# Decoder trunk with experts on one core: another order of the value tiles, an eleven-step choice of experts, slots released behind a second round, parameters fetched in attention

## What is computed

```python
for l in range(DEPTH):                       # DEPTH = 2, 256 tokens, width 1024
    h = rms_norm(x, norm1_g[l])
    proj = h @ w_in[l]                       # 1024 -> 3072: q, k, v of two attention groups
    o_da = diff_attention(q, k, v, lam)      # softmax(a) - lam * softmax(b), causal
    o_sb = stick_breaking_attention(...)     # log-sigmoid scores with a reverse cumulative sum
    x = x + concat([norm(o_da), norm(o_sb)]) @ w_out[l]
    h2 = rms_norm(x, norm2_g[l])
    x = x + hierarchical_moe(h2, ...)        # best group of 4, then the best two of its 8 experts
                                             # expert: (silu(h2 @ w_gate) * (h2 @ w_up) * weight) @ w_down
```

## Time and profile before

| | |
|---|---|
| median of 3 runs | 782.0 us (781.1 to 782.14) |
| the profiled execution, its own time | 780.52 us |
| its span, first to last instruction | 778.7 us |
| PE, DVE, ACT busy | 671.7, 306.5, 127.3 us |
| mean granted TensorE clock | 0.949 of full |
| bytes moved by DMA | 240.10 MB, mean 308 GB/s |

### The profile page before, as it was taken

One profiled execution on the slowest core, in us unless ns is written; L12 is line 12 of the kernel. 1 busy time (PEld: TensorE's weight loads), 2 busy tenths in 40 slices (PEclk: granted clock), 3 DMA queues, 4 the chain that ended last, 5 costly groups with the idle time before them and its releaser, 6 DMA issues.

```text
span 778.7 us, 12467 instructions
## 1 busy us (share of the span) xinstructions
PE 671.7 (86%) x4708; PEld 367.3 (47%) x4709; DVE 306.5 (39%) x675; ACT 127.3 (16%) x318; POOL 9.0 (1%) x19
## 2 busy tenths in 40 slices
PE   8998999977879797595899989999888888885596
PEld 5444556475535254253344454564745534443252
DVE  0346634262442343322324377322633425432323
ACT  3113632111000100000031155212100000000000
POOL 0000000001000000000020000000000000000000
PEclk9999999999989999898999999999999999997889
DMA  8698127528996899999999740284289969999996
GB/s 308 215 396 342 63 74 295 226 109 253 374 421 263 369 421 421 423 421 421 400 362 391 290 152 12 108 332 170 93 343 422 421 266 424 422 423 420 423 417 228
DMA packets 53206, 240.10 MB, mean 308 GB/s; under 512 B 7792, under 2 KB 8080, under 8 KB 29616
## 3 DMA queue, kind: packets, MB, share of 16 engines
q1 hardware_dynamic: 52560, 238.61, 76.8%
q0 software_dynamic: 608, 0.99, 1.1%
HBM read 238.54 MB, written 1.05 MB: 308 GB/s over the span
## 4 chain that ended last, share of the span: by engine, by line
PE 61%; DMA 27%; DVE 4%; issue 3%; SPq 2%; ACT 1%; DVEq 1%; ACTq 1%
DMA wbuf<-in_w_up 20%; PE bank L1106 20%; PE bank L1256 10%; PE bank L1203 7%; DMA wbuf<-in_w_down 6%; PE bank L1288 5%; PE bank L1231 5%; PE bank L1300 4%; PE bank L1267 2%; PE bank L1163 1%; PE bank L1150 1%; SPq L349 1%; DMA wbuf<-in_w_in 1%; PE bank L1183 1%; PE bank L1176 1%
## 5 line engine op out<-in xcount | busy, mean ns | idle before, releaser
L1106 PE MATMUL bank<-wbuf,hTbuf 128*128 128x512 f32 x384 | 169.8, 599 | 2.0 <-DMA wbuf<-in_w_in 1.6
L1256 PE MATMUL bank<-wbuf,qkT 128*32 128x256 f32 x2048 | 128.4, 411 | 47.0 <-DMA wbuf<-in_w_up 47.0
L1256 PEld LDWEIGHTS bank<-wbuf,qkT 128*32 128x32 f32 x2048 | 68.5, 119 | 110.1 <-DMA wbuf<-in_w_up 50.8
L1106 PEld LDWEIGHTS bank<-wbuf,hTbuf 128*128 128x128 f32 x384 | 72.7, 192 | 89.3 <-issue 87.4
L1231 PE MATMUL bank<-qkT,xn 128*128 128x128 f32 x512 | 68.0, 297 | 10.0 <-issue 10.0
L1231 PEld LDWEIGHTS bank<-qkT,xn 128*128 128x128 f32 x512 | 64.8, 209 | 17.3 <-issue 17.1
L1288 PE MATMUL bank<-wbuf,qkT 128*32 128x512 f32 x512 | 58.6, 595 | 16.2 <-DVE qkT L828 7.6
L840 DVE TENSOR_TENSOR x_sb<-x_sb,bank 128x512 f32<-128x512 f32 x72 | 49.5, 688 | 50.3 <-PE bank L1300 50.3
L1203 PE MATMUL bank<-wbuf,hTbuf 128*128 128x512 f32 x128 | 56.0, 593 | 0.0
L1288 PEld LDWEIGHTS bank<-wbuf,qkT 128*32 128x32 f32 x512 | 15.0, 110 | 50.1 <-issue 33.7
L539 ACT COPY qkT<-bank 128x512 f32<-128x512 f32 x16 | 9.4, 585 | 173.0 <-PE bank L1231 160.6
(11 more groups left out here) (205 smaller groups left out, 589.7 us busy)
## 6 DMA issues: line engine op xcount, KB each, us to landing
wbuf<-in_w_gate SPq DMA_DIRECT2D x64, 1024.0 KB, 14.3
wbuf<-in_w_up SPq DMA_DIRECT2D x64, 1024.0 KB, 18.7
wbuf<-in_w_down SPq DMA_DIRECT2D x56, 1024.0 KB, 13.9
wbuf<-in_w_in SPq DMA_DIRECT2D x24, 1024.0 KB, 14.3
wbuf<-in_w_out SPq DMA_DIRECT2D x8, 1024.0 KB, 6.2
wbuf<-in_w_down SPq DMA_DIRECT2D x16, 512.0 KB, 9.1
x_sb<-in_x SPq DMA_DIRECT2D x2, 512.0 KB, 4.6
out<-x_sb SPq DMA_DIRECT2D x2, 512.0 KB, 2.6
```

The lines of the kernel that those rows point to most:

```text
L1106: last = MM(ps[PROJ_BANK[i][t]][:, :], hT[:, k, t * P:(t + 1) * P], block_rows(i, k), start=(k == 0), stop=(k == KC - 1))
L1256: last = MM(ps[bank][j * SLOTS:(j + 1) * SLOTS, 0:FF], hgT[:, k, j * SLOTS:(j + 1) * SLOTS], halves[:, at[j], k, :], start=(k == 0), stop= ...
```

## The change

- **Value tiles.** On TensorE, tile (4, 0) moves ahead of `transpose_qk(l, 3)` and of the first `da_transpose`; (5, 0) takes the old place of (4, 0), and (4, 1) that of (5, 0), so no projection stands any more between the last `cumulate` and `attend(l, 0)`. ScalarE's evacuations move accordingly.
- **Router.** The gain of the second norm is multiplied into the router weights once (`wr_scaled`) and into the gathered tokens, so x is copied plainly; ScalarE makes `xn`; each tile's router products are split in halves that start with their half of the transpose; the logits of both tiles have banks of their own. The choice of experts takes eleven steps. It masks the other groups' experts with `NEG` instead of finding a second maximum in every group. The first one-hot tile goes to `ranks` while the second is still being found, with `keep_clock(5)` between; `keep_clock(4)` behind `ranks` is gone.
- **Slots.** `second_and_further_rounds` runs the second round straight, and the loop only if there are more than 64 tokens (on ScalarE and VectorE; TensorE keeps the nested loops). `gate_used` and `up_used` are raised behind the gate exponential of the last round. SP issues lane 3 of the ups ahead of the next gates from the third set on.
- **Parameters.** In layer 0, block 0's first half goes ahead of x's second tile, whose transpose moves inside the first projection; the parameters of the router and the output norms go behind block 3. Layer 1's first-norm and head gains are fetched by GpSimd in layer 0's attention. The broadcast copy `g2` (512 KB per layer) is dropped.

```diff
+        def second_and_further_rounds(eng, most, begun, one):
+
+            eng.reg_add(begun, begun, 1)
+            one(eng.snap(begun), 1)
+            with eng.If(most > 2 * SLOTS):
+                with eng.Fori(2, ROUNDS) as r:
+                    with eng.If(most > r * SLOTS):
+                        eng.reg_add(begun, begun, 1)
+                        one(eng.snap(begun), r)
...
+                    if g > 1:
+                        sp_.wait_ge(up_used, l * SETS + g)
+                        load_up(l, g, LANES - 1)
                     if g + 1 < SETS:
                         sp_.wait_ge(gate_used, l * SETS + g)
                         for j in range(LANES):
                             load_gate(l, g + 1, j)
-                    sp_.wait_ge(up_used, l * SETS + g)
-                    load_up(l, g, LANES - 1)
+                    if g == 1:
+                        sp_.wait_ge(up_used, l * SETS + g)
+                        load_up(l, g, LANES - 1)
...
+            load_half(0, 0, 0)
             sp_.dma_start(x_sb[:, 1, :], x[0, P:2 * P, :]).then_inc(x_in[1], 16)
-            for i in range(IN_BLOCKS):
+            load_half(0, 0, 1)
+            for i in range(1, IN_BLOCKS):
                 load_block(0, i)
                 if i == 1:
                     sp_.dma_start(cst[:, C_GE:], const[:, C_GE:]).then_inc(const_in, 16)
                     for dst, src in gains(0):
                         sp_.dma_start(dst, src).then_inc(gains_in[0], 16)
+                if i == 3:
...
-                pool.wait_ge(routed, l)
+                pool.wait_ge(qkT_ps, l * 8)
...
+            def last_norm(l):
+
+                act.wait_ge(x_attn, l * 2 * TT + 3)
+                nc.scalar.activation(y[:, 0:HALF], x_sb[:, 1, 0:HALF], ACT.Square, accum_out=ssq[:, 2:3])
+                act.drain()
+                nc.scalar.activation(ssq[:, 3:4], ssq[:, 2:3], ACT.Copy, scale=1.0 / D, bias=EPS)
+                act.wait_ge(x_attn, l * 2 * TT + 4)
+                nc.scalar.activation(y[:, HALF:], x_sb[:, 1, HALF:], ACT.Square, accum_out=ssq[:, 1:2])
+                hT_plain(2 * l + 1, 1)
+                act.drain()
+                nc.scalar.activation(rstd[:, 1:2], ssq[:, 1:2], ACT.Ln, bias=ssq[:, 3:4], scale=1.0 / D)
+                act.drain()
+                nc.scalar.activation(rstd[:, 1:2], rstd[:, 1:2], ACT.Exp, scale=-0.5)
+                act.drain().then_inc(norm_r, 1)
...
+            def normed(t):
+                nc.scalar.activation(xn[:, t, :].rearrange("p (k c) -> p c k", k=KC),
+                                     x_sb[:, t, :].rearrange("p (c k) -> p c k", k=KC), ACT.Copy,
+                                     scale=rstd[:, t:t + 1]).then_inc(xn_ready, 1)
...
-                nc.scalar.copy(dst[:, 4:8, :], ps[1][:, :].rearrange("p (k s) -> p k s", k=4)).then_inc(s["hg_a"], 1)
+                for k in range(4):
+                    last = nc.scalar.activation(dst[:, 4 + k, :], ps[1][:, k * P:(k + 1) * P], ACT.Copy,
+                                                scale=g2T[:, 4 + k:5 + k])
+                last.then_inc(s["hg_a"], 1)
...
-                    act.wait_ge(more["act_out"], m)
+                    with act.If(most <= r * SLOTS + SLOTS):
+                        act.sem_inc(gate_used, 1)
+                        act.sem_inc(up_used, 1)
                     with act.If(most > r * SLOTS + SLOTS):
+                        act.wait_ge(more["act_out"], m)
...
-                    further_rounds(act, most, begun, further)
-                    act.sem_inc(gate_used, 1)
-                    act.sem_inc(up_used, 1)
+                    second_and_further_rounds(act, most, begun, further)
...
-                    further_rounds(dve, most, begun, further)
+                    second_and_further_rounds(dve, most, begun, further)
...
+                V.tensor_tensor(wr[:, :, :], wr[:, :, :], g2T[:, :].unsqueeze(2).broadcast_to([P, KC, GROUPS + EXPERTS]),
+                                ALU.mult).then_inc(wr_scaled, 1)
...
+                gl, el = lg[:, :, 0:GROUPS], grouped(lg[:, :, GROUPS:])
...
+                V.tensor_reduce(best, el, AX.X, ALU.max)
+                gap()
+                for t in range(TT):
...
+                V.scalar_tensor_tensor(grouped(em[:, :, :]), each(others, PER_GROUP), NEG, el, ALU.mult, ALU.add)
+                V.tensor_tensor(grouped(oh1[:, :, :]), grouped(oh1[:, :, :]), each(first_at, PER_GROUP), ALU.is_equal)
+                V.tensor_tensor(group, group, wide(rs[:, 7, :], GROUPS), ALU.is_equal)
+                gap()
+
+                V.scalar_tensor_tensor(ev[:, :, :], oh1[:, :, :], 3 * NEG, em[:, :, :], ALU.mult, ALU.add)
+                V.tensor_tensor(grouped(oh1[:, :, :]), grouped(oh1[:, :, :]), each(group, PER_GROUP), ALU.mult)
+                gap().then_inc(rt_first, 1)
...
+                V.tensor_reduce(rs[:, 2, :], ev[:, :, :], AX.X, ALU.max)
+                V.tensor_reduce(rs[:, 1, :], em[:, :, :], AX.X, ALU.max)
+                gap()
+                for t in range(TT):
+                    V.scalar_tensor_tensor(oh2[:, t, :], ev[:, t, :], rs[:, 2, t:t + 1], rev, ALU.is_equal, ALU.mult)
+                V.tensor_tensor(rs[:, 4, :], rs[:, 2, :], rs[:, 1, :], ALU.subtract).then_inc(rt_diff, 1)
+                gap()
+                V.tensor_reduce(rs[:, 7, :], oh2[:, :, :], AX.X, ALU.max)
+                gap()
+                V.tensor_tensor(oh2[:, :, :], oh2[:, :, :], wide(rs[:, 7, :], EXPERTS), ALU.is_equal)
+                gap().then_inc(rt_second, 1)
                 V.tensor_tensor(asg[:, 0:TT, :], oh1[:, :, :], oh2[:, :, :], ALU.add)
...
+                        if l == 0 and t == 0:
+                            pe.wait_ge(x_in[1], 16)
+                            transpose_x(1)
...
+            def router(l, t, half):
+                pe.wait_ge(hT_a if half else hT_d, (2 * l + 1) * TT + t + 1)
...
+                pe.wait_ge(rt_first, l + 1)
+                MM(ps[5][:, 0:TT * EXPERTS], tri_lt, oh1[:, :, :], start=True, stop=False)
+                MM(ps[5][:, EXPERTS:2 * EXPERTS], ones, oh1[:, 0, :], start=False, stop=False)
+                keep_clock(5)
+                pe.wait_ge(rt_second, l + 1)
+                MM(ps[5][:, 0:TT * EXPERTS], tri_lt, oh2[:, :, :], start=False, stop=False)
+                MM(ps[5][:, EXPERTS:2 * EXPERTS], ones, oh2[:, 0, :], start=False, stop=True).then_inc(pos_ps, 1)
+                pe.wait_ge(rt_total, l + 1)
+                MM(ps[6][:, 0:EXPERTS], ones, asg[:, TT, :], start=True, stop=True).then_inc(total_ps, 1)
...
-                pe.wait_ge(proj_out, l * 12 + 8)
+                proj_tile(l, 4, 0)
+                transpose_qk(l, 3)
                 da_transpose(l, 0)
                 da_transpose(l, 1)
-                transpose_qk(l, 3)
                 pe.wait_ge(qkT_d, l * 4 + 4)
                 pe.wait_ge(qkT_a, l * 4 + 4)
                 sb_scores(l, 4, 5)
                 sb_scores(l, 0, 1)
-                proj_tile(l, 4, 0)
+                proj_tile(l, 5, 0)
                 pe.wait_ge(daT_out, l * 3 + 1)
                 da_transpose(l, 2)
                 if l == 0:
...
                 cumulate(l, 5)
                 pe.wait_ge(daT_out, l * 3 + 3)
                 sb_scores(l, 2, 3)
-                proj_tile(l, 5, 0)
+                proj_tile(l, 4, 1)
                 for w in range(4):
                     cumulate(l, w)
-                proj_tile(l, 4, 1)
                 attend(l, 0)
...
+                pe.wait_ge(wr_scaled, l + 1)
+                router(l, 0, 0)
                 pe.wait_ge(x_attn, l * 2 * TT + 4)
                 transpose_x(1)
-                router(l, 0)
-                router(l, 1)
+                router(l, 0, 1)
+                router(l, 1, 0)
+                router(l, 1, 1)
                 keep_clock(12)
                 ranks(l)
-                keep_clock(4)
+                pe.wait_ge(xn_ready, (l + 1) * TT)
```

More of the change, by code:

```diff
@@ L595, in _ @@
                 act.wait_ge(g1_in[l], 16)
[L596 to L599 removed]
+                if l == 0:
+                    hT_half(0, 0, g1T)
+                    for t in range(TT):
                         act.wait_ge(x_in[t], 16)
[L601 removed]
+                        norm(0, t)
+                    hT_half(0, 1, g1T)
+                else:
+                    for t in range(TT):
+                        hT_half(2 * l, t, g1T)
+                    for t in range(TT):
                         act.wait_ge(x_tile[t], l * SETS)
[L603 removed]
+                        norm(l, t)
                 act.wait_ge(lam_dot, l + 1)
@@ L646, in _ @@
                 act.wait_ge(par_in[l], N_PAR)
-                for t in range(TT):
-                    act.wait_ge(x_attn, l * 2 * TT + 2 * (t + 1))
-                    norm(l, t)
-                    hT_half(2 * l + 1, t, g2T)
+                act.wait_ge(x_attn, l * 2 * TT + 2)
+                norm(l, 0)
+                normed(0)
+                hT_plain(2 * l + 1, 0)
```

(24 more changed lines are left out.)

118 lines of the change are left out of this document (48 added, 70 removed).

## The result

The changed kernel takes 786.42 us (median of 15 runs, 782.57 to 789.24), the kernel before 782.43 us (15 runs, 780.17 to 788.29): ratio 1.0043, 95% interval 1.0023 to 1.0063. The forecast of 751.2 us and its range of 743 to 766 were wrong, and wrong in sign. The profiled execution took 786.42 us for a span of 784.6.

A forecast was written before the change was run, and what follows sets the result against it. TensorE's list bounds attention and router, the weight stream the experts, with two holes of about 17 us together. Gains of 16.0 experts, 6.8 value tiles, 6.0 router and 2.0 start sum to 30.8: 751.2 us, range 743 to 766.

The forecast's parts named there:

- rival B: VectorE's grown loop code stalls twice per layer, 4 times 3.5 us, giving 765 us; chance 0.08.
- I had said 9.5: Layer 0's experts: earlier release and ups close the hole in the weight stream, 10.0 us by count, 9.5 taken.
- layer 1's hole: Layer 1's experts: the weight stream's rest before the gates of 633.89 closes, 7.6 us by count, 7.1 taken.
- the release's 6.2 us: Third set: slots released right behind the second round's exponential, so the next gates are issued 6.2 us earlier.
- The 2 us assumed for the up: Layer 1's third set: lane 3's up arriving earlier moves the gates by 2 us, under half of layer 0's wait.
- The value tiles: Attention: moved projection covers TensorE's waits and avoids half clock around the second transpose_qk; net 3.4 us per layer, bounds 1 to 4.6.
- The router: Router to first gather: earlier logits, fewer selection steps, gather nearer full clock; 3.0 us per layer, bounds 1.5 and 3.5.
- The start: Layer 0's first projection: its weights have half a megabyte less ahead of them; 2.0 us, bounds 0.5 and 2.6.
- A: Expert stages: the third set's downs come no earlier, so the next wait takes half the hole; 763 us, chance 0.10.
- C: Attention and router bring half: new waits as long as old, half clock stays; 759 us, chance 0.08.
- D: SP's in-order list: gates wait for the ups, 12 sets lose 3.15 us each; 789 us, slower, chance 0.03.
- E: Expert streams: no change that can be told, because both layers' streams are bound elsewhere; chance 0.02.

The follow-up runs named there:

- the one-copy kernel: Changed kernel with nested loops again, one copy of the further round's code, on VectorE and ScalarE: 757.47 us, ratio 0.9678.
- its three places: Changed kernel as is (786.42 us), and with 64 or 128 memsets added at VectorE's start: 785.25 us (1.0039) and 787.82 us (1.0055).
- the front alone: Changed kernel with one copy of the further round, old slot release and old order of the ups, leaving start, value tiles and router: 769.36 us, ratio 0.9828 or 764.85, 0.9784.
- experiment 9: Changed kernel with one copy of the further round on both engines, and the old order of value tiles on TensorE and ScalarE: ratio 0.9828.
- experiments 2 and 4: Changed kernel with lane 3 of the ups behind the gates again: 788.16 us, 1.0056; kernel before with only the new ups order: 778.88 us, 0.9926.

## Why the prediction was wrong, step by step

**The step that failed** is rival B's, and the sentence under it: "Nothing of the kind shows on VectorE now, and once the stream runs it has slack." I had counted that the loop grows from 237 to 278 rows, had a row with such a stall on TensorE, and gave the case four stalls of 3.5 us and a chance of 0.08. That no such row stood on VectorE was no evidence: the loop was still short enough, and the edge lay between its length and the new one. So the sum held nothing for the grown loop, where the runs show 28.6 us, and the range held at most B's 14. The three sizes were wrong as well: six turns, not four; 5.2 us each and not 3.5 (and 2.8 more in layer 1); and no slack. The slack failed because the stall sits ahead of the selection, the selection ahead of the gather, and the gather ahead of the downs, whose use asks for the next loads; a stalled layer thus lost most of what it stalled. In layer 0 the three stalls add 15.8 us, and the experts took 222.0 against 207.9 us in the one-copy kernel; in layer 1 they add 23.9 us, and the experts took 230.3 against 212.2.

The Trainium skill (Runtime: NRT & Kernel Launch, Instruction fetch mechanics) says that a taken branch to outside the two held blocks of 256 instructions stalls the engine for a fetch. The direction holds: the stalls stand at the loop's backward branch, and one or two packets on the instruction queue come within each of them and within no other turn. The size of the window doesn't explain the rest. By it, as an estimate from the page's figure, 345 to 354 instructions would lie within two blocks at many places; counted from where the loops start in the built programs, no placing of the block edges makes all six loops of the changed kernel at its three places reach into a third block. Yet all six stalled, while the kernels of 297 to 317 never did. The page has no price; here it was 5.2 us for a turn with one packet and 8.2 to 9.3 with two, while the load queues moved some 420 GB/s.

**What hit.** TensorE never waited for an up in the third set again. The release follows the exponential at once. ScalarE's timeline of the changed kernel shows

```profile
237.57 0.38 ACT L593 ACTIVATE qkT<-bank 128x256 f32<-128x256 f32 x1 [5.92 <-PE bank L1329]
```

and SP's

```profile
238.34 2.14 SPq L348 DMA_DIRECT2D wbuf<-in_w_gate  x4
```

which are 0.4 us apart instead of 6.2. Without the loop's stalls layer 0's experts shorten from 219.5 to 207.9 us; I had said 9.5, it was 11.6.

**Mis-sized: layer 1's hole.** I took 7.1 us; the stage shortened by 1.1. Of the two shifts of the gates that I added up, the release's 6.2 us, carried over from layer 0, came as said (74.7 to 68.5 us after the first gate product). The 2 us assumed for the up did not come at all (68.5 to 68.9). And a shift the other way was missing from the sum: with the front alone the gates already came 2.4 us later (72.3 to 74.7), and the stage took 215.9 us instead of 213.3. That the front's own gain is what delays them, as the early loads of layer 1 had less time to run ahead, fits these numbers but was not tried.

**The value tiles.** The mechanism was right and the size near: one pair of transposes follows the projection without a wait, and the scores run at full clock, 2.03 us for what took 3.49. The changed kernel, TensorE:

```profile
79.70 1.04 PE L1185 MATMUL bank<-cst,wbuf 128*128 128x128 f32 x8
80.58 1.04 PE L1217 MATMUL bank<-cst,wbuf 128*128 128x128 f32 x8
81.54 2.03 PE L1209 MATMUL bank<-qkT 64*128 64x128 f32 x24
...
93.27 1.14 PE L1209 MATMUL bank<-qkT 64*128 64x256 f32 x8 [0.29 <-ACT wbuf L569]
...
108.07 2.00 PE L1242 MATMUL bank<-wbuf 128*128 128x64 f32 x16 [0.55 <-ACT wbuf L573]
```

The kernel before has two more rows at this place that bear on it:

```profile
74.17 0.66 PE L1158 MATMUL bank<-cst,wbuf 128*128 128x128 f32 x4 [0.53 <-DVEq L744]
...
82.19 7.13 PE L1106 MATMUL bank<-wbuf,hTbuf 128*128 128x512 f32 x16
```

I had left out the 0.53 us ahead of `da_transpose`. The new waits are 0.55 us in `attend`, which I had at 0.7, and 0.29 ahead of the later scores, for which I had taken 0.5. The terms are 2.12 + 0.77 + 0.53 + 1.46 (3.49 less 2.03), less 0.55 and 0.29: 4.0 us. That is what attention gained in each layer against the kernel before (layer 0's 4.2 less 0.2 of the start), where I had said 3.4 with bounds of 1 and 4.6.

With the old order in the new kernel (experiment 9), the same place reads

```profile
73.16 0.66 PE L1217 MATMUL bank<-cst,wbuf 128*128 128x128 f32 x4 [0.52 <-DVEq L796]
75.94 1.06 PE L1185 MATMUL bank<-cst,wbuf 128*128 128x128 f32 x8 [2.12 <-DVE dmax L777]
77.77 3.79 PE L1209 MATMUL bank<-qkT 64*128 64x128 f32 x24 [0.77 <-ACT qkT L543]
81.48 8.30 PE L1165 MATMUL bank<-wbuf,hTbuf 128*128 128x512 f32 x16
```

Here the half clock reached further than in the kernel before: the scores took 3.79 us instead of 3.49, and the projection behind them began at the half clock too and took 8.30 us instead of 7.13. So undoing the order costs more in the new kernel than the order gained over the old one, and the 11.7 us of experiment 9 (with some 4 us either way) are not a measure of my term. Why the half clock lasts longer there stays open.

**The router** gave 2.5 and 2.9 us where I said 3.0. The first gather takes 3.81 us at full clock, where it was 5.47. **The start** gave 0.2 in the one trace where I said 2.0. Among fourteen traces with the new start the first `transpose_qk` begins between 36.6 and 42.1 us, and in three with the old one between 37.4 and 39.6: an effect of 2 us cannot be told there, and my term came from one trace as if it could.

**Rivals A, C, D, E.** None came true in the forecast's form. D had the right sign for the wrong cause: gates behind the ups cost nothing (experiments 2 and 4). Without the second copy the kernel takes 757.5 us, which is 6 above my 751.2 and inside the range; the range failed by the one case that I left too cheap.

## What to carry to other kernels

Count an engine's loop in instructions of the built program, skipped branches included, before and after an edit that duplicates code in it, and look at the packets of the instruction queue and the "issue" time at the loop's first instruction: code that never runs can cost a stall at every turn. An engine that is busy 38% of the span has no slack if its first step of each turn stands ahead of what the bounding chain needs next. If a special case needs code of its own, take something else out of the loop, or undo the copy and keep the rest: here one copy of the round, with all other parts of the change, runs in 757.5 us and beats both kernels.

## What the runs showed of the hardware

A turn of VectorE's loop took 2.53 to 2.59 us of registers and branches, at 251 to 317 instructions, in every kernel. At 345 to 354 it took 7.6 to 8.1 us at some places and 10.6 to 11.9 at others, or still 2.6 to 2.8, and for one body moving it by 64 instructions swapped which of two layers stalls. The instruction queue then moved 8 KB packets, 16 more for each stalled layer: one in the idle time of each turn of 7.6 to 8.1 us, two, 5.0 us apart, in each of 10.6 to 11.9, and none in the others. What exactly decides between these places stays open: neither the length alone nor the whole loop's place does. A stall of this kind also costs clock on TensorE: the gather behind it took 6.11 us instead of 3.81.
